# The overflow loop of a 32-expert feed-forward: one block of 64 rows a turn instead of two, with the two column halves of TensorE on the two halves of one expert's columns

## What is computed

```python
g_prob = softmax(h @ w_gr + b_gr); p_grp, grp = top_k(g_prob, 1)       # 4 groups of 8 experts
top_v, top_i = top_k(expert_logits_of_the_group, 2)                    # 2 experts a token
weight = p_grp * softmax(top_v); expert = grp * 8 + top_i
y = (silu(xr @ w_gate[e]) * (xr @ w_up[e])) @ w_down[e]                # 1024 -> 512 -> 1024
out[token] += weight * y                                               # then norm, gate, residual
```

## Time and profile before

| | us |
|---|---|
| median of 3 runs | 2270.03 |
| lowest and highest | 2264.95 and 2270.65 |
| profiled execution | 2264.99 |
| its span | 2263.2 |
| granted TensorE clock in it, mean | 0.917 |

### The profile page before, as it was taken

One profiled execution on the slowest core, in us unless ns is written; L12 is line 12 of the kernel. 1 busy time (PEld: TensorE's weight loads), 2 busy tenths in 40 slices (PEclk: granted clock), 3 DMA queues, 4 the chain that ended last, 5 costly groups with the idle time before them and its releaser, 6 DMA issues.

```text
span 2263.2 us, 20180 instructions
## 1 busy us (share of the span) xinstructions
PE 1906.7 (84%) x7320; PEld 1035.5 (46%) x7320; DVE 827.4 (37%) x1438; ACT 514.0 (23%) x785; POOL 361.8 (16%) x400
## 2 busy tenths in 40 slices
PE   6898888888889788898988989999946878888782
PEld 1455544544545565666656644444432333333331
DVE  1444354454444556654566552221331000000003
ACT  2221231231231424443244320000330000000003
POOL 0111011011021244432444310000001000000000
PEclk9899998898998999999999999999967999888997
DMA  6113113113122111111111235531356999999994
GB/s 248 41 38 94 32 43 102 46 28 93 46 75 57 37 38 37 37 46 37 30 44 28 83 136 171 167 111 56 124 218 267 428 431 429 429 429 430 429 409 166
DMA packets 153549, 350.16 MB, mean 155 GB/s; under 512 B 14066, under 2 KB 104395, under 8 KB 140443
## 3 DMA queue, kind: packets, MB, share of 16 engines
q1 hardware_dynamic: 144282, 332.68, 39.0%
q10 hardware_dynamic: 4176, 8.41, 1.0%
q0 software_dynamic: 5040, 8.40, 1.0%
HBM read 346.09 MB, written 13.32 MB: 159 GB/s over the span
## 4 chain that ended last, share of the span: by engine, by line
PE 60%; DMA 17%; DVE 8%; issue 7%; ACT 5%; POOL 2%; SPq 0%; DVEq 0%; ACTq 0%; POOLq 0%
PE bank L620 11%; PE bank L477 7%; PE bank L1966 5%; DMA arena<-in_w_up_dram 5%; PE bank L1484 4%; DMA arena<-in_w_gate_dram 4%; PE bank L674 4%; PE bank L1096 4%; PE bank L482 3%; PE bank L1503 3%; PE bank L1486 2%; PE bank L1984 2%; PE bank L697 2%; PE bank L1156 2%; DMA stay<-in_w_up_dram 2%
## 5 line engine op out<-in xcount | busy, mean ns | idle before, releaser
L620 PE MATMUL bank<-stay,arena 128*128 128x512 f32 (+1 forms) x704 | 250.3, 516 | 24.8 <-DVE arena L786 22.6
L1966 PE MATMUL bank<-arena 128*64 128x512 f32 x832 | 204.5, 649 | 41.6 <-DMA arena<-in_w_up_dram 31.9
L620 PEld LDWEIGHTS bank<-stay,arena 128*128 128x128 f32 x704 | 139.6, 199 | 140.6 <-issue 115.3
L477 PE MATMUL bank<-arena 128*128 128x512 f32 x384 | 181.1, 627 | 16.4 <-ACT arena L489 15.3
L1966 PEld LDWEIGHTS bank<-arena 128*64 128x64 f32 x832 | 71.2, 149 | 173.4 <-issue 171.9
L2028 DVE TENSOR_TENSOR arena<-arena,bank 128x512 f32<-128x512 f32 x17 | 11.7, 688 | 323.5 <-PE bank L1966 323.5
L477 PEld LDWEIGHTS bank<-arena 128*128 128x128 f32 x384 | 77.1, 205 | 110.5 <-issue 89.7
L674 PE MATMUL bank<-arena,stay 128*128 128x512 f32 x256 | 120.8, 628 | 0.0
L1984 PE MATMUL bank<-arena 128*64 128x512 f32 x384 | 90.0, 623 | 17.1 <-issue 9.0
L1156 PE MATMUL bank<-arena 128*128 128x128 f32 x448 | 68.1, 304 | 39.1 <-DVE arena L1268 35.9
L1286 DVE TENSOR_TENSOR arena<-arena 128x256 f32<-128x256 f32 x112 | 77.4, 731 | 63.7 <-ACT arena L1062 57.6
(11 more groups left out here) (377 smaller groups left out, 2856.3 us busy)
## 6 DMA issues: line engine op xcount, KB each, us to landing
arena<-in_w_gate_dram SPq DMA_DIRECT2D x26, 2048.0 KB, 25.1
arena<-in_w_up_dram SPq DMA_DIRECT2D x26, 2048.0 KB, 27.7
arena<-in_w_down_dram SPq DMA_DIRECT2D x24, 2048.0 KB, 27.2
arena<-in_w_in_dram SPq DMA_DIRECT2D x64, 512.0 KB, 4.0
arena<-in_w_ada_dram SPq DMA_DIRECT2D x12, 2048.0 KB, 9.8
stay<-in_w_down_dram SPq DMA_DIRECT2D x10, 2048.0 KB, 25.0
stay<-in_w_gate_dram SPq DMA_DIRECT2D x8, 2048.0 KB, 26.0
stay<-in_w_up_dram SPq DMA_DIRECT2D x8, 2048.0 KB, 27.2
```

What stands on the lines that cost most here:

```text
L477: mm = pe.matmul(b[:, :], w[:, k, :], src[:, k, 0:LAT], start=(k == 0), stop=(k == KT - 1))
L620: mm = pe.matmul(ps[:, 0:n], w[:, k, :], hT[:, k, o:o + n], start=(k == 0), stop=(k == KT - 1))
L1966: mm = pe.matmul(b[cols, :], xgT[r][:, k, cols], w[u][:, k, :], start=(k == 0), stop=(k == KT - 1))
```

## The change

The loop now takes one block of 64 rows a turn (`nover` turns, at least 1). The two column halves of the array, which before held the two experts of a pair, both hold the same 64 rows and work on the two halves of one expert's columns: gate columns 0 to 255 and 256 to 511, and so for up and for the 1024 columns of down. Each product so has half the streamed columns or half the matmuls. The product of gate and up is turned with 8 matmuls against halves of the identity in place of 4 transposes. Of each chunk one load of 2048 KB is made. The result has 64 rows in two halves of 512 columns on 128 partitions, and is scattered in half rows of `y_dram`. The table needs the rows of an overflow block on both partition halves, so it is built from two products: bank 5 for the 16 pairs, bank 6 for the overflow blocks (the same for both halves).

Lines of the changed kernel in the rows below: L1697 and L1700 table, L1973 to L2009 the main loop's `rows`, `up`, `turn_gated` and `down`, L1990 `up_halves`, L2046 the new turning, L2055 the new down product.

```diff
-        NB = NSUB // 2 + 1
+        NB = PAIRS + NOV + 1
+        NHOT = E + NOV + 1
...
             for par in range(2):
                 for j in range(NT):
-                    mm = pe.matmul(bank[5][par * SLOT:(par + 1) * SLOT, 0:NB], soh[:, j, :],
-                                   boh[:, j, :].rearrange("p (b u) -> p u b", u=2)[:, par, :],
+                    rows = slice(par * SLOT, (par + 1) * SLOT)
+                    pe.matmul(bank[5][rows, 0:PAIRS], soh[:, j, :],
+                              boh[:, j, 0:E].rearrange("p (b u) -> p u b", u=2)[:, par, :],
+                              start=(j == 0), stop=(j == NT - 1))
+                    mm = pe.matmul(bank[6][rows, 0:NB - PAIRS], soh[:, j, :], boh[:, j, E:NHOT],
                                    start=(j == 0), stop=(j == NT - 1))
...
-            L(dve.tensor_scalar(novi, binc[:, E - 1:E], 1.0, 2.0, ALU.add, ALU.max))
-            dve.tensor_scalar(npair, novi, 1, None, ALU.arith_shift_right).then_inc(s_rv, 1)
+            L(dve.tensor_scalar(upperhalf, pidf[:, 0:1], float(SLOT), None, ALU.is_gt))
+            dve.tensor_scalar(nover, binc[:, E - 1:E], 1.0, None, ALU.max).then_inc(s_rv, 1)
...
-            L(dve.tensor_copy(tbl, bank[5][:, 0:NB]))
+            own.mark(dve.tensor_copy(tbl[:, 0:PAIRS], bank[5][:, 0:PAIRS]))
+            L(dve.tensor_copy(tbl[:, PAIRS:NB], bank[6][:, 0:NB - PAIRS]))
...
-            L(dve.tensor_copy(sidx, tbl))
+            own.mark(dve.tensor_scalar(inv, tbl, 2.0, upperhalf, ALU.mult, ALU.add))
+            L(dve.tensor_copy(sidx[:, 0:PAIRS], tbl[:, 0:PAIRS]))
+            L(dve.tensor_copy(sidx[:, PAIRS:NB], inv[:, PAIRS:NB]))
...
-            n = sp.value_load(npair[0:1, 0:1], min_val=1, max_val=NOV // 2)
+            n = sp.value_load(nover[0:1, 0:1], min_val=1, max_val=NOV)
             with sp.Fori(0, n) as i:
-                pair = []
-                for u in range(2):
-                    e = sp.value_load(bexp[0:1, bass.ds(i * 2 + u, 1)], min_val=0, max_val=E - 1)
-                    pair.append(bass.ds(e, 1))
+                e = sp.value_load(bexp[0:1, bass.ds(i, 1)], min_val=0, max_val=E - 1)
+                def load_one(kind):
+                    sp.dma_start(weights_of(OVER + kind)[0], expert_source(kind, bass.ds(e, 1))).then_inc(s_w[(OVER + kind) % 4], 16)
                 sp.wait_ge(s_d, PAIRS - 1)
                 sp.wait_ge(s_g, PAIRS + i)
-                load(PAIRS, 0, pair)
+                load_one(0)
...
+            def scatter_halves(index):
+                pool.indirect_dma_start(out=y_dram.rearrange("t (u d) -> (t u) d", u=2),
+                                        out_offset=bass.IndirectOffsetOnAxis(ap=index, axis=0),
+                                        in_=yb[0][:, 0:512], in_offset=None,
+                                        bounds_check=4 * LAT - 1, oob_is_err=False).then_inc(s_sc[0], 16)
...
+            def up_halves(chunk, loaded, b, done):
+                w = weights_of(chunk)[0]
+                pe.wait_ge(s_w[chunk % 4], loaded)
+                for k in range(KT):
+                    for u in range(2):
+                        mm = pe.matmul(b[u * SLOT:(u + 1) * SLOT, 0:256], xgT[0][:, k, 0:SLOT], w[:, k, u * 256:(u + 1) * 256],
+                                       start=(k == 0), stop=(k == KT - 1))
+                mm.then_inc(done, 1)
...
             with pe.Fori(0, n) as i:
                 rows(0, PAIRS * 8 + 16 + i * 16, PAIRS + i)
...
-                turn_gated(0, PAIRS + i)
+                for f in range(FT):
+                    for u in range(2):
+                        rows_u = slice(u * SLOT, (u + 1) * SLOT)
+                        mm = pe.matmul(bank[4][rows_u, f * SLOT:(f + 1) * SLOT], g[:, f, :], ident[:, rows_u],
+                                       start=True, stop=True)
...
-                down(OVER + 2, landed(OVER + 2) + i * 32, PAIRS + i)
+                for f in range(FT):
+                    for u in range(2):
+                        mm = pe.matmul(bank[5][u * SLOT:(u + 1) * SLOT, :], guT[:, f, 0:SLOT], w[:, f, u * 512:(u + 1) * 512],
+                                       start=(f == 0), stop=(f == FT - 1))
...
-                gated(0, PAIRS + i)
-                rows(0, PAIRS + i, PAIRS * 8 + i * 16)
+                dve.tensor_tensor(gu[0][:, 0:256], gu[0][:, 0:256], bank[3][:, 0:256], ALU.mult).then_inc(s_gu, 1)
+                dve.wait_ge(s_d, PAIRS + i + 1)
+                dve.wait_ge(s_sc[0], PAIRS * 8 + i * 16)
+                dve.tensor_copy(yb[0][:, 0:512], bank[5][:, :]).then_inc(s_yb, 1)
```

More of the change, by code:

```diff
@@ L1619, in build @@
         bexp = take(NOV).bitcast(I32)
-        npair = take(1).bitcast(I32)
+        nover = take(1).bitcast(I32)
         idg = take(1).bitcast(U32)
@@ L1642, in build @@
         cnti = take(E).bitcast(I32)
-        novi = take(1).bitcast(I32)
+        upperhalf = take(1)
         tE = take(NT, E)
@@ L1647, in build @@
         soh = take(NT, SLOT)
-        boh = take(NT, 2 * NB)
+        boh = take(NT, NHOT)
         cmpb = take(NOV, E)
@@ L1841, in experts_sync @@
                     sp.wait_ge(s_rv, TABLES)
-            n = sp.value_load(npair[0:1, 0:1], min_val=1, max_val=NOV // 2)
+            n = sp.value_load(nover[0:1, 0:1], min_val=1, max_val=NOV)
             with sp.Fori(0, n) as i:
-                pair = []
-                for u in range(2):
-                    e = sp.value_load(bexp[0:1, bass.ds(i * 2 + u, 1)], min_val=0, max_val=E - 1)
-                    pair.append(bass.ds(e, 1))
+                e = sp.value_load(bexp[0:1, bass.ds(i, 1)], min_val=0, max_val=E - 1)
+                def load_one(kind):
+                    sp.dma_start(weights_of(OVER + kind)[0], expert_source(kind, bass.ds(e, 1))).then_inc(s_w[(OVER + kind) % 4], 16)
                 sp.wait_ge(s_d, PAIRS - 1)
                 sp.wait_ge(s_g, PAIRS + i)
-                load(PAIRS, 0, pair)
+                load_one(0)
                 sp.wait_ge(s_u, PAIRS + i)
-                load(PAIRS, 1, pair)
+                load_one(1)
                 sp.wait_ge(s_d, PAIRS + i)
-                load(PAIRS, 2, pair)
+                load_one(2)
             sp.wait_ge(s_sc[0], PAIRS * 8 + n * 16)
@@ L1905, in experts_gpsimd @@
                 pool.tensor_tensor(pad[:, 0:1], pad[:, 0:1], pad[:, 0:1], ALU.mult)
-                scatter(0, ids)
+                scatter_halves(ids)
             pool.wait_ge(s_xg[0], PAIRS * 8 + 16 + n * 16)
@@ L1935, in experts_scalar @@
                 gated_columns(b)
[L1936 removed]
+            n = act.value_load(nover[0:1, 0:1], min_val=1, max_val=NOV)
             with act.Fori(0, n) as i:
@@ L1940, in experts_scalar @@
                 act.wait_ge(s_gut, PAIRS + i)
-                gate(PAIRS + i, 0)
+                act.wait_ge(s_g, PAIRS + i + 1)
+                act.activation(gu[0][:, 0:256], bank[2][:, 0:256], ACT.Silu).then_inc(s_sig, 1)
                 act.wait_ge(s_d, PAIRS + i)
-                gated_columns(PAIRS + i)
+                act.wait_ge(s_gut, PAIRS + i + 1)
+                act.copy(guT[:, :, 0:SLOT], bank[4][:, 0:256].rearrange("p (f c) -> p f c", f=FT)).then_inc(s_guc, 1)
             for cc in range(LCH):
@@ L2011, in experts_tensor @@
                 pe.wait_ge(s_sig, PAIRS + i)
[L2012 removed]
+                up_halves(OVER, landed(OVER - 4) + 16 + i * 16, bank[2], s_g)
                 pe.wait_ge(s_gu, PAIRS + i)
[L2014 removed]
+                up_halves(OVER + 1, landed(OVER - 3) + 16 + i * 16, bank[3], s_u)
                 pe.wait_ge(s_guc, PAIRS + i)
[L2016 to L2018 removed]
+                pe.wait_ge(s_gu, PAIRS + i + 1)
+                g = gu[0][:, 0:256].rearrange("p (c f) -> p f c", f=FT)
+                for f in range(FT):
[3 more added lines that the diff above has]
+                                       start=True, stop=True)
+                mm.then_inc(s_gut, 1)
+                pe.wait_ge(s_yb, PAIRS + i)
+                w = weights_of(OVER + 2)[0]
+                pe.wait_ge(s_guc, PAIRS + i + 1)
+                pe.wait_ge(s_w[(OVER + 2) % 4], landed(OVER - 2) + 16 + i * 16)
+                for f in range(FT):
+                    for u in range(2):
+                        mm = pe.matmul(bank[5][u * SLOT:(u + 1) * SLOT, :], guT[:, f, 0:SLOT], w[:, f, u * 512:(u + 1) * 512],
+                                       start=(f == 0), stop=(f == FT - 1))
+                mm.then_inc(s_d, 1)
         ylc = arena[:, 0:4096].rearrange("p (j d) -> p j d", d=D)
```

12 lines of the change are left out of this document (7 added, 5 removed).

## The result

| | before | changed |
|---|---|---|
| median, us (22 runs each) | 2270.33 | 2277.58 |
| lowest and highest, us | 2264.95, 2277.79 | 2270.62, 2285.69 |
| profiled execution, us | 2264.99 | 2279.12 |

The ratio is 1.0034, 95% interval 1.0025 to 1.0043, which is +7.7 us (5.7 to 9.8). The forecast was +9.4 on the profiled execution. Single executions of one kernel lie up to 13 us (before) and 15 us (changed) apart, so differences between profiles are read stretch by stretch.

A forecast was written before the change was run, and what follows sets the result against it. The prediction took weights to bound the main loop and PE the overflow turn, with serial ends. Overflow +6.1, scatter -0.3, table +3.2 and DVE +0.4 gave +9.4 us: a median of 2279 us, range 2269 to 2289.

The forecast's parts named there:

- Number of turns: Overflow loop: the last scatter's packets show two blocks, so the changed loop runs two turns where one ran before.
- Table: Table product at the end of the routing: 64 records for 32 at 0.100 us each, nothing hiding it, +3.2 us.
- DVE: DVE steps around the table: three operations more, +0.4 us, from 0.2 to 0.66.
- Scatter: Final scatter after the overflow: half rows with half the bytes, 3.0 us for 3.29, -0.3 us.
- Overflow turns: Overflow loop: two turns pay for the same products and twice for all between them, +6.1 us, 4.4 to 8.1.
- the wait for the gather: Ahead of the second turn's transposes: gather lands after 13.6 us, so PE waits 1 to 3 us.
- between up and down: In each overflow turn: smaller operands save what the new turning takes, 3.0 us against 2.97 before.
- the products' own errors: Products of each overflow turn: gate and up 3.6 us each, down 3.55 us, with the halves alternating.
- "PE is the bound, not the weights": Old overflow turn: PE bounds it, with three products of 7.09 us each in its 27.4 us.
- rival 4: Last pair's up and down: at full clock, overflow starts 3.4 us earlier, sum +6.0, no measurable difference; chance 0.16.
- Rivals 1 and 2: Overflow: second turn's weights late, +7.8 us, chance 0.10; halves of gate and up not overlapping, +14.4 us, chance 0.04.
- Rival 3: Overflow products: throttled to a mean clock of 0.81, +5.1 us, in all +14.5; chance 0.08.

The follow-up runs named there:

- experiment 5: Changed kernel with both 2048 KB loads of each chunk issued in each overflow turn, as before the change; ratio to before 1.0137.
- experiment 2: Changed kernel with its table built by 16 matmuls of 33 columns in place of 32 of 16 and 17; ratio to before 1.0002.
- experiments 6 and 7: Changed kernel with all matmuls of the lower column half before the upper, 1.0082; changed kernel with at least 3 overflow turns, 1.0096.
- (4): Kernel before, with no edit, profiled twice more; 2270.83 and 2271.99 us.
- both kernels of 3: The kernel of experiment 2 with its table product issued twice, 1.0036; the kernel before with its table product issued three times, 1.0032.
- experiment 1: Kernel before with its table product issued a second time into bank 6, 32 matmuls in place of 16; ratio 1.0024.
- the third kernel of 8: The kernel of experiment 2 with each overflow turn's rows gathered, transposed and copied during the turn ahead; ratio to before 0.9998.
- the first two kernels of 8: Kernel before with the overflow turn's rows gathered, transposed and copied one step earlier, 1.0005; the same with its weights also issued early, 0.9997.

## Why the prediction was right, and where it was not

- **Number of turns**, read from the packets of one scatter: right, two scatters now.
- **Table**, +3.2: measured +3.39, at a clock that stayed at 0.50 throughout. The price per record was right and no cover appeared. The Trainium skill (TensorEngine Tiling (Array Packing), Instruction Overhead) gives each matmul an overhead of some 60 cycles; counted for each record at 1.2 GHz, as an estimate, that would have been half of it.
- **DVE**, +0.4: +0.45. **Scatter**, -0.3: -0.60.
- **Overflow turns**, +6.1: +3.52. This term was mis-sized, and 3.52 is itself against the shortest of three profiles of the old loop (30.02, 30.46 and 33.86 us); against their mean it is +2.1. From the first transposes to DVE's last copy I had 34.9 us, measured 32.35 (2209.03 to 2241.38). Of the 2.56 between, 1.83 was the wait for the gather, which never came: it landed after 9.9 us, before the turn ended. I had priced it from a row taken with a full queue, though the change itself thins that queue; experiment 5 shows this by filling it again. The other 0.73 was mostly between up and down (2.73 and 2.51 us in the two turns, for 3.0); the products' own errors (7.13 for 7.2, 3.65 for 3.55) nearly cancel.
- **"PE is the bound, not the weights"**, of the old turn: wrong in general. In the one profile I had, its up product waited 0.79 us, and I took it for a PE chain. Six runs show its start held by the weights. The old turn thus swallows much of a late or early start: with main loops of 490.6 (third profile) and 495.5 us (table thrice) its last scatter was issued at 524.4 and 524.7 us after SP's first issue. The new one, a chain with half-size loads, does not: with 490.4 (experiment 2) and 494.9 us its loop took 33.53 and 33.54, and the scatter was issued at 523.9 and 528.4. This is why the new loop is exposed to the next point.
- **The clock of the last pair** was my rival 4, with the sign turned: I saw 3.4 us to gain, and the changed kernel lost 1.1 more there (9.88 for 8.78 in up). Over three profiles either way (the changed kernel with experiments 6 and 7) the main loop is 495.0 against 491.6, +3.4 us in untouched code, which my sum had at nothing: 1.8 until the last up product starts, from the late rise of the clock in the first gate product (4), and 1.6 in the last two products. The steps' 6.76 and this would make +10.2, above the measured 5.7 to 9.8; part of it the old turn's slack gave back before, since the last scatter's issue came 522.1, 522.6 and 524.4 us after the routing's end then, and 528.4 now: +5.4 on the means, and with table, DVE and scatter +8.6. So the total of +9.4 came near the measured +7.7 in part by luck: an overflow priced too high stood against a main loop that lost time for a reason that I had not priced.
- Rivals 1 and 2 (late weights, no overlap) did not occur. Experiments 5 and 6 force their like, with twice the loads and with the halves in a row, and cost 23 and 11 us. Rival 3 did not occur: all products of both turns ran at full clock.

What stays open: what in the change makes the main loop slower, and whether it is the longer table. Main loops of 494.9 to 495.5 us came in five profiles with 64 or more records (changed kernel, both kernels of 3, 6 and 7) and 493.6 in a sixth (5); the kernel before and experiment 2, with 32, had 490.4 to 492.2. But experiment 1 has 64 records and 490.7, and the third kernel of 8 has 32, and its pair 15 ended at 493.5. The late rise of the clock in the first gate product does not follow the table's length either: SP's second issue comes at 24.8 to 25.0 us in the kernel before, experiment 1 (64 records) and the first two kernels of 8, and at 26.3 to 26.8 in all others, experiment 2 and the third kernel of 8 (32 records) among them. At the other end, the last pair's up product took 8.78 us or more in the thirteen profiles in which it had waited 3.56 to 3.90 us for its weights, and 7.09 in the one in which it had waited 2.36 (experiment 2). No run varies these waits by themselves.

## What to carry over

A loop turn over half the work halves only what streams; the transposes, copies and hand-overs between engines (here 5.1 of 15.8 us) are paid again each turn. So before splitting turns ask what their fixed part is and whether the old turn had a wait that hid its own. Price a transfer by a row taken under the load that will be there after the change, not before it. A term of a few us needs more than one profile of the kernel before: the same overflow turn of the same program differed by 3.8 us among three. Where small matmuls stand alone between two engines' steps, count them: each costs the same whatever its few columns.

## What was not expected of the hardware

- An f32 record with 64 stationary columns at granted clock 0.50 cost 0.10 us for 16, 25 and 33 columns; the clock did not rise in 10.07 us of such products (experiment 3).
- Products with all matmuls of one column half ahead of all of the other cost 0.181 us a record of 256 columns, alternating ones 0.111; another place of the program, which uses one half only, had 0.225.
- The granted clock's course differed by program and repeated within it only in part: the last up product took 9.88, 9.84 and 9.79 us in the three with the same instructions up to there and 8.78 in all three profiles of the kernel before, but the down product after it took 8.78, 8.78 and 7.09 us in those three.
- A rise of the clock from 0.50 to 1.00 that came 2 to 3 us later within one product, while the DMA engines stood still, went with a last up product, bound by its weights, that began some 1.5 to 2 us later 450 us on.
